# Branch products of the merge: three passes on rounded parts and remainders in place of native float32 products

## The reference, cut to what matters

```
u = hn @ w_in                                  # 27 column tiles of 128 for the mixers, 32 for the merge gates
ya, yb, yc, yd = rwkv7(...), hgrn2(...), retention(...), rglru(...)     # (1024, 256) each, times silu of a gate
merge_gates = sigmoid(u[merge columns]).reshape(B, T, 4, 1024)
merged = sum(merge_gates[:, :, b] * (branches[b] @ w_branch[b]) for b in range(4))
h = x + gate * (merged @ w_out);  return rmsnorm(h, final_g)
```

## Time and profile before

| | |
|---|---|
| device time, median of three | 1259.23 us (1258.71 to 1263.32) |
| the profiled execution, first to last instruction | 1258.2 us |
| TensorE busy | 1170.9 us, 93% |
| TensorE weight loads | 867.5 us, 69% (beside the matmuls) |
| VectorE busy | 664.7 us, 53% |
| ScalarE busy | 293.6 us, 23% |
| GpSimd busy | 300.4 us, 24% |
| branch products (L551) | 256 records, 119.8 us |
| mean granted TensorE clock | 0.963 of full speed |

### The profile page before, as it was taken

One profiled execution on the slowest core, in us unless ns is written; L12 is line 12 of the kernel. 1 busy time (PEld: TensorE's weight loads), 2 busy tenths in 40 slices (PEclk: granted clock), 3 DMA queues, 4 the chain that ended last, 5 costly groups with the idle time before them and its releaser, 6 DMA issues.

```text
span 1258.2 us, 21439 instructions
## 1 busy us (share of the span) xinstructions
PE 1170.9 (93%) x9156; PEld 867.5 (69%) x9156; DVE 664.7 (53%) x1088; ACT 293.6 (23%) x423; POOL 300.4 (24%) x271
## 2 busy tenths in 40 slices
PE   1899999899889999999999999999999998999997
PEld 1687786676567677667767777776666666776886
DVE  5656835843642342453443118558787768433353
ACT  3615115113111120220220134223222330001221
POOL 0443532211241111111111233321111213553000
PEclk9699999999989999999999999998889989999999
DMA  9311112101001101010110121111100115421221
GB/s 380 113 51 34 51 50 68 34 21 30 14 22 31 33 25 31 23 34 23 31 35 18 29 65 42 34 44 30 36 22 23 30 29 203 136 76 51 100 85 51
DMA packets 80094, 70.33 MB, mean 56 GB/s; under 512 B 4096, under 2 KB 72960, under 8 KB 78976
## 3 DMA queue, kind: packets, MB, share of 16 engines
q1 hardware_dynamic: 74528, 49.50, 12.6%
q10 hardware_dynamic: 5472, 19.47, 4.2%
HBM read 64.76 MB, written 4.19 MB: 55 GB/s over the span
## 4 chain that ended last, share of the span: by engine, by line
PE 75%; DVE 17%; ACT 3%; issue 2%; DMA 2%; SPq 0%; POOL 0%; DVEq 0%; ACTq 0%
PE bank L508 45%; PE bank L891 7%; PE bank L551 5%; PE bank L727 2%; DVE stage L1722 2%; PE bank L733 2%; PE bank L731 2%; DVE stage L1725 1%; DMA slots<-in_w_mod 1%; PE bank L841 1%; DVE slots L1789 1%; DVE slots L1604 1%; DVE slots L1361 1%; DVE slots L1414 1%; PE bank L704 1%
## 5 line engine op out<-in xcount | busy, mean ns | idle before, releaser
L508 PE MATMUL bank<-hn_hi,w_hi 128*128 128x512 f32 x944 | 398.3, 422 | 8.1 <-ACT slots L960 3.1
L508 PE MATMUL bank<-hn_lo,w_hi 128*128 128x512 f32 x944 | 375.1, 397 | 0.0
L508 PE MATMUL bank<-hn_hi,w_lo 128*128 128x512 f32 x944 | 374.2, 396 | 0.0
L439 POOL CAST w_hi<-w_raw 128x512 fp32r<-128x512 f32 x118 | 82.4, 698 | 819.9 <-PE bank L508 785.1
L508 PEld LDWEIGHTS bank<-hn_hi,w_hi 128*128 128x128 f32 x944 | 181.4, 192 | 57.6 <-issue 8.9
L508 PEld LDWEIGHTS bank<-hn_hi,w_lo 128*128 128x128 f32 x944 | 181.2, 192 | 40.2
L508 PEld LDWEIGHTS bank<-hn_lo,w_hi 128*128 128x128 f32 x944 | 182.1, 193 | 37.1 <-issue 3.6
L441 POOL TENSOR_TENSOR w_lo<-w_raw,w_hi 128x512 fp32r<-128x512 f32 x118 | 162.3, 1376 | 9.5
L551 PE MATMUL bank<-slots,w_branch 128*128 128x512 f32 x256 | 119.8, 606 | 3.2 <-DVE slots L1517 3.2
L982 ACT ACTIVATE stage<-bank 128x512 f32<-128x512 f32 x64 | 38.2, 597 | 244.4 <-PE bank L508 211.2
L551 PEld LDWEIGHTS bank<-slots,w_branch 128*128 128x128 f32 x256 | 47.6, 191 | 49.5 <-issue 46.6
(11 more groups left out here) (273 smaller groups left out, 1440.8 us busy)
## 6 DMA issues: line engine op xcount, KB each, us to landing
w_raw<-in_w_in SPq DMA_DIRECT2D x118, 256.0 KB, 2.8
slots<-in_w_mod SPq DMA_DIRECT2D x8, 1024.0 KB, 8.7
slots<-in_x SPq DMA_DIRECT2D x8, 512.0 KB, 7.9
w_branch<-in_w_branch SPq DMA_DIRECT2D x32, 128.0 KB, 2.5
slots<-in_w_mod ACTq DMA_DIRECT2D x8, 512.0 KB, 5.3
slots<-in_w_out ACTq DMA_DIRECT2D x8, 512.0 KB, 6.3
xr<-in_x ACTq DMA_DIRECT2D x8, 512.0 KB, 3.6
out<-xr ACTq DMA_DIRECT2D x8, 512.0 KB, 2.6
```

Of the source, the lines that this page charges most:

```text
L439: nc.gpsimd.tensor_copy(w_hi[p][:, :, :], w_raw[p][:, :, :]).then_inc(s_w_hi_ready, 1)
L508: last = mm(o, w[p][:, k4, :], h[:, k, n * HALF:(n + 1) * HALF], start=(p == 0 and k4 == 0 and q == 0), stop=(p == 1 and k4 == 3 and q == 2))
```

## The change

The branch products get the form that the input projection has. For each half of 512 tokens six fp32r passes take the place of two native matmuls (two blocks k, three passes each). For this both operands are split:

- the weights: GpSimd, after it has split the gate columns of a merge tile, rounds `w_branch` into `w_branch_hi` and subtracts it into `w_branch_lo` (128x256 each, 32 times). `w_branch_hi` lies over `lru_w`, `w_branch_lo` over the raw buffer itself. TensorE waits for `s_w_branch_ready` in place of the landing.
- the branch outputs: for D, A and B ScalarE rounds (`cast_y`: two times 128x1024 each for D and A, four times 128x512 for B), for C GpSimd does; the remainder is always GpSimd's (`split_y`), written over the output itself. TensorE waits for `s_y_lo_ready` in place of `s_y_ready`.
- where these stand: ScalarE's of D at L1014, ahead of the sigmoids L1020; of A ahead of its HGRN loop; of B at L1179, ahead of the issue of the last weight transfers. GpSimd's of D and A after the weights of merge tiles 0 and 16; of B after those of merge tile 24; of C behind its product at L457.

A new tile `y_hi` (128 x 4 x 1024) moves the addresses behind it. The two semaphores of the rope tables become one, and the program asks for a smaller scratch area for DMA descriptors.

```diff
+Y_HI = {3: 0, 2: 2, 0: 0, 1: 2}
+Y_LO_COUNT = {3: (2, 2), 2: (4, 4), 0: (6, 6), 1: (8, 10)}
...
+            def split_y(b, j, cols, y_hi_count):
+                pool.wait_ge(s_y_hi_ready, y_hi_count)
+                lo = y_lo[Y_SLOT[b]][:, j, cols]
+                nc.gpsimd.tensor_tensor(lo, slot(Y_SLOT[b] + j)[:, cols], y_hi[:, Y_HI[b] + j, cols].bitcast(F32),
+                                        ALU.subtract).then_inc(s_y_lo_ready, 1)
...
+                if BULK[bi] >= MG:
+                    b, m = MERGE_TILES[merge]
+                    h, z = merge % 2, merge // 2
+                    pool.wait_ge(s_w_branch_landed[h], 16 * (z + 1))
+                    nc.gpsimd.tensor_copy(w_branch_hi[h][:, :, :], w_branch[h][:, :, :]).then_inc(s_pool_step, 1)
+                    pool.wait_ge(s_pool_step, after(s_pool_step))
+                    nc.gpsimd.tensor_tensor(w_branch_lo[h][:, :, :], w_branch[h][:, :, :],
+                                            w_branch_hi[h][:, :, :].bitcast(F32), ALU.subtract)\
+                        .then_inc(s_w_branch_ready, 1)
+                    if merge in (0, 16):
+                        for j in range(2):
+                            split_y(b, j, slice(0, T), (1 if merge == 0 else 5) + j)
+                    elif merge == 24:
+                        for q in range(4):
+                            split_y(b, q % 2, slice(q // 2 * HALF, (q // 2 + 1) * HALF), 7 + q)
+                    merge += 1
...
                     nc.gpsimd.tensor_tensor(slot(6 + j), slot(18 + j), slot(6 + j), ALU.mult).then_inc(s_y_ready[2], 1)
+                    pool.wait_ge(s_y_ready[2], j + 1)
+                    nc.gpsimd.tensor_copy(y_hi[:, Y_HI[2] + j, :], slot(6 + j)).then_inc(s_y_hi_ready, 1)
+                    split_y(2, j, slice(0, T), 3 + j)
...
-                    pe.wait_ge(s_w_branch_landed[mi % 2], 16 * (mi // 2 + 1))
-                pe.wait_ge(s_y_ready[b], 2 * (n + 1) if b == 1 else 2)
+                    pe.wait_ge(s_w_branch_ready, mi + 1)
+                pe.wait_ge(s_y_lo_ready, Y_LO_COUNT[b][n])
...
                 for k in range(2):
-                    last = mm(bank[2 + n][:, :], w_branch[mi % 2][:, k, :], slot(y + k)[:, n * HALF:(n + 1) * HALF],
-                              start=(k == 0), stop=(k == 1))
+                    for q, (w, h) in enumerate(((w_h, hi), (w_h, lo), (w_l, hi))):
+                        last = mm(bank[2 + n][:, :], w[:, k, :], h[:, k, :], start=(k == 0 and q == 0),
+                                  stop=(k == 1 and q == 2))
...
+            def cast_y(b, j, cols):
+                nc.scalar.activation(y_hi[:, Y_HI[b] + j, cols], slot(Y_SLOT[b] + j)[:, cols], ACT.Copy)\
+                    .then_inc(s_y_hi_ready, 1)
+
             act.wait_ge(s_y_ready[3], 2)
+            for j in range(2):
+                cast_y(3, j, slice(0, T))
...
             evac(2)
+            act.wait_ge(s_y_ready[0], 2)
+            act.wait_ge(s_br_done, 16)
+            for j in range(2):
+                cast_y(0, j, slice(0, T))
...
             merge_gate()
-
-            act.wait_ge(s_y_ready[1], 4)
+            act.wait_ge(s_br_done, 32)
+            for q in range(4):
+                act.wait_ge(s_y_ready[1], q + 1)
+                cast_y(1, q % 2, halves(q // 2))
```

27 lines of the change are left out of this document (20 added, 7 removed).

## The result

The changed kernel takes 1280.14 us (median; 1278.13 to 1285.08) beside 1260.29 us for the kernel before on the same chip: a ratio of 1.0162, 95% interval 1.014 to 1.0184. It is slower by some 20 us. The forecast was 1262.5 us with a range from 1249.5 to 1273; the third rival, slower by the clock, had 1277.5 us. The profiled execution after spans 1279.1 us (1258.2 before), at a mean granted clock of 0.949 (0.963 before).

What follows compares the result with a forecast made beforehand. TensorE, busy 93% of the span, was taken as the bound, with VectorE ending waits at chunk ends; -10.8 us of gains against held-up engines and clock made +3.5 on 1258.2, median 1262.5 us, range 1249.5 to 1273.

Steps and rivals of the forecast that it cites:

- the third rival: Clock falls at all six RWKV chunk ends and for one more stretch per HGRN chunk: 1277.5 us; chance 0.20.
- The levels, -5.0 us: Levels of RWKV's inverse, chunks 1 to 7: TensorE sets the pace, 14 pieces gain 0.354 us each.
- the fifth rival: Branch products' passes take 0.25 us each because operands alternate between buffers; gain gone, 1272 us; chance 0.02.
- Ends of chunks: no gain from the shorter product: RWKV chunks 1 to 6, HGRN chunks 0 to 6: VectorE ends later already, shorter products only lengthen the wait; gain 0.
- Held-up VectorE in RWKV, +3.0 us: Ends of RWKV chunks 1 to 6: new GpSimd instructions make VectorE end 0.5 us later each; bounds 0 to 6.6.
- HGRN, +5.6 and +2.0 us: Seven HGRN chunk ends: VectorE 0.8 us later each, +5.6 (0 to 7.7); lower clock, +2.0 (0 to 7).
- The tail, -5.0 - 0.3 us: Merge tiles 25 to 31 gain 0.71 us each, -5.0; merge tile 24, started on VectorE's word, gains 0.3.
- the end of chunk 7, -0.5 us: End of RWKV's chunk 7: no `prep` follows, so the shorter product was taken to gain 0.5 us.
- D's casts, +1.7 us: ScalarE's two casts ahead of the sigmoids, before RWKV: everything behind them moves 1.7 us later; bounds 0 and 2.1.
- The clock in RWKV, +2.0 us: Ends of RWKV chunks 1 to 6: waits of about 1.95 us bring one clock fall of six; bounds 0 to 12.
- the ten passes assumed: After a clock fall at an RWKV chunk end: some ten passes each 0.2 us longer, 2.0 us a fall.
- 9.2 us of 22.6: Share of TensorE's saving over all 32 merge tiles lying in 13 at chunk ends, where VectorE ends later: gain 0.

Runs made afterwards that it cites:

- e2: Changed kernel with GpSimd splitting the branch weights only for the first two merge tiles, so not the layer's output: 1256.31 us (0.9976).
- e4: Changed kernel with GpSimd's split of the branch weights half a tile earlier, behind part 0 of the gate columns: 1261.43 us (1.0012).
- e1: Changed kernel with all splits kept but the native float32 branch products of the kernel before: 1270.41 us (1.0084).
- e3: Changed kernel with ScalarE's two casts of branch D moved behind the sigmoids: 1273.84 us (1.0104).
- e10: Kernel before with one VectorE product in `prep` written three times more at the ends of RWKV chunks 1 to 6: 1273.82 us (1.0112).
- e12: Changed kernel with seven fp32r passes repeated in the levels of each of RWKV's chunks 1 to 7, lengthening the chunk: 1277.76 us (1.0143).
- e9: Kernel before with one VectorE product in `prep` written twice more at the ends of RWKV chunks 1 to 6: 1266.04 us (1.0055).
- e11: Changed kernel with one filler piece moved from the start of each RWKV and HGRN chunk to its end: 1252.38 us (0.9936).

## Why the prediction was wrong, point by point

- **The levels, -5.0 us.** Right. Kernels without falls show it: 48.3 us a chunk against 48.9 (e2, e4), so -4.2 us in seven. The pass at 0.234 us rather than 0.227 makes it 0.6 us a tile where 0.7 was put. With 0.25 us a pass, the fifth rival, the gain would not have been gone, as was said: three passes would take 0.75 us and still gain 0.108 of the 0.177 us, and by the same sum that rival comes to some 1267 us and not 1272. It is gone at 0.286 us a pass.
- **Ends of chunks: no gain from the shorter product.** Right: e2 lengthens the wait by 0.66 us and gains nothing there.
- **Held-up VectorE in RWKV, +3.0 us.** Right. e1 has 49.4 us against 48.9, six times 0.5.
- **HGRN, +5.6 and +2.0 us.** 7.6 together, 7.3 measured. That the splits make it is shown by e2 (176.5 us without them, 176.1 before); how it divides between VectorE and the clock is not: time at half speed goes from 37.5 us (830 to 1030 us before) to 51.2 us (850 to 1055 us after), and part of that lies beside VectorE, as e2 has 44.4 us of it (830 to 1030 us) and loses nothing.
- **The tail, -5.0 - 0.3 us, and the end of chunk 7, -0.5 us.** -6.5 measured for the rest, and -5.4 and -5.8 in e2 and e4. Chunk 7 to HGRN's first takes 172.6 us in these two against 173.8, so -1.2, of which 0.6 are the levels and 0.6 its end. Right in mechanism and about in size.
- **D's casts, +1.7 us.** The direct part is right (TensorE's wait 1.27 to 2.86 us), the price is not: 6.3 us by e3, 5.3 by the means of the profiles, above the bound of 2.1. I had priced the wait and not the clock behind it, though I did so in the next stage.
- **The clock in RWKV, +2.0 us.** This is the step that failed. The wait was forecast to 0.05 us (1.95; 1.90 came), and it was said that one such wait lies between a wait that is followed by half speed and those that are not the earlier trace rows. Then "I take one fall in RWKV's six" chose a value near the end without falls, with no row for it. There were six, at 2.5 us each: 15 us. The bound of 12 was too low as well, since every second fall costs 3.3 us and not the 2.0 of the ten passes assumed. What the prediction had no term for is the place of the wait in time.
- **Putting it together.** With 15 in place of 2.0 and 6 in place of 1.7 the sum is +20.8 us, against 20.9 between the two profiled spans. The other terms add up as they stand.
- **The range.** The third rival was the mechanism and at 1277.5 us nearly the size. The range stopped in its middle, at 1273. No row spoke for a middle: with equal waits and equal chunks the rows gave no reason why some ends should fall and others not. Ends without a fall among equal waits do occur (two falls of six in e10 and in e12, one in e9), but in e10 and e12 those began 1.47 to 2.83 us behind a grid instant, a place that no row of before showed, so six falls had to lie inside the range, or the 0.20 outside it as a whole.

VectorE beside GpSimd went as the earlier trace rows had it, where L1543 ends 0.28 us after L441. In the trace after, the instructions of VectorE with two SBUF inputs that start while L471 and L473 run also end 0.28 us after them (L1601 at 522.64, L1604 at 523.50, against 522.36 and 523.22). In the kernel before both took 0.42 us; here they took 0.50 and 0.83 us.

What stays open: from which length on a wait can be followed by a fall, and why the place on the grid parts those with one from those without. Waits of 0.78, 1.25, 1.38, 1.42 and 1.44 us had none in six ends each; of those of 1.69 us (e9) one had, at 0.25 us behind a grid instant, and those at 0.49 and 0.89 us had none. And each kernel has one profile, so how the number of falls varies between executions of one kernel is not shown.

## What to carry to other kernels

Where an edit lengthens a wait of TensorE between blocks of dense matmuls, price two things: the wait, and a fall of the clock behind it. Here 28 of 36 waits of 1.87 to 2.16 us had one, at 1.7 or 3.3 us each by the estimate for the changed kernel. In a loop put a fall at every end inside the range, unless a trace shows waits of that length, at several places in time, without one. This loop's six falls went in three ways: by filler at the wait (e11, none left), by moving the other engine's work away from the instructions that end it (e4, none left), or (by luck alone) by another length of the loop (e12, two left). What an operation saves on TensorE was given back where another engine ends the wait: e2 lengthens it by 0.66 us there and gains nothing. By the prediction's count 9.2 us of 22.6 were such. Filler moved to such ends can change that: in RWKV's chunks 1 to 6 the change with its splits moved is worth 3.0 us without it (296.9 to 293.9) and 5.9 us with it (291.0 to 285.1). Over the whole kernel it is worth the same, 8.4 and 8.5 us, so that a gain in one stage isn't yet a gain of the kernel. And compare with the kernel before that has the same filler, or the filler's gain is put down to the change.
